# Long convolutions by quarters: fewer transform products, with sums, differences and gates on GpSimd

## The reference, cut to what matters

```
u = dwconv3(h @ w_in, conv_w, conv_b)              # 512 x 3072
v, x1, x2 = split(u)
filt = (sin-MLP(positions) @ f_w3) * decay         # forward and backward filters
k2 = concat(fwd, 0, reversed bwd); k2 /= sum(|k2|)
zc = v
for o in range(2):                                  # two orders
    y  = irfft(rfft(zc, n=1024) * rfft(k2[o]))[:512]
    zc = gates[o] * (y + skip[o] * zc)
out = zc @ w_out
```

## Time and profile before

| what | value |
|---|---|
| median of the runs shown | 2739.63 us |
| the profiled execution: its own time, its span | 2741.72 us, 2739.7 us |
| TensorE busy | 2678.6 us (98%) |
| VectorE busy | 1723.7 us (63%) |
| ScalarE busy | 1024.8 us (37%) |
| GpSimd busy | 136.6 us (5%) |

### The profile page before, as it was taken

How to read it: one execution, slowest core, us unless ns; L and a number is a source line. 1 busy time by engine, 2 the same in 40 slices (tenths; PEclk the granted TensorE clock), 3 DMA queues, 4 the chain that set the end, 5 groups by cost and what they waited for, 6 DMA issues and landing times.

```text
span 2739.7 us, 35605 instructions
## 1 busy us (share of the span) xinstructions
PE 2678.6 (98%) x14500; PEld 2158.4 (79%) x14500; DVE 1723.7 (63%) x2544; ACT 1024.8 (37%) x1488; POOL 136.6 (5%) x171
## 2 busy tenths in 40 slices
PE   8999899999998999999899999999999999999999
PEld 6777688888775688888775788888888888888888
DVE  4388677474677567574757567575664988644434
ACT  4355444232435444242427543232432223432323
POOL 0000200000033200000003200000000000000000
PEclk9999999999999999999999999999999999999999
DMA  4432144343321134343220046454231111332221
GB/s 173 118 76 66 48 134 148 128 138 96 91 89 62 51 128 149 118 150 98 89 89 1 32 135 204 150 186 137 97 121 62 32 35 46 102 114 93 92 86 53
DMA packets 247210, 275.27 MB, mean 100 GB/s; under 512 B 9287, under 2 KB 213575, under 8 KB 247048
## 3 DMA queue, kind: packets, MB, share of 16 engines
q1 hardware_dynamic: 216696, 217.67, 24.9%
q10 hardware_dynamic: 30352, 55.31, 6.3%
HBM read 265.36 MB, written 7.34 MB: 100 GB/s over the span
## 4 chain that ended last, share of the span: by engine, by line
PE 87%; DVE 8%; ACT 3%; issue 2%; DMA 0%; ACTq 0%; DVEq 0%
PE ps L571 24%; PE ps L573 23%; PE ps L572 23%; PE ps L1291 3%; PE ps L1323 2%; PE ps L1044 2%; PE ps L1061 1%; PE ps L1248 1%; DVE sb L2407 1%; DVE sb L2405 1%; PE ps L1269 1%; DVE sb L1983 1%; PE ps L1158 1%; PE ps L1078 1%; PE ps L630 1%
## 5 line engine op out<-in xcount | busy, mean ns | idle before, releaser
L571 PE MATMUL ps<-sb 128*128 128x512 f32 (+1 forms) x3332 | 1256.7, 377 | 14.3 <-ACT sb L1449 3.1
L573 PE MATMUL ps<-sb 128*128 128x512 f32 (+1 forms) x3332 | 1235.7, 371 | 0.0
L572 PE MATMUL ps<-sb 128*128 128x512 f32 (+1 forms) x3332 | 1235.4, 371 | 0.0
L571 PEld LDWEIGHTS ps<-sb 128*128 128x128 f32 x3332 | 628.0, 188 | 145.0 <-issue 27.8
L573 PEld LDWEIGHTS ps<-sb 128*128 128x128 f32 x3332 | 628.2, 189 | 108.7
L572 PEld LDWEIGHTS ps<-sb 128*128 128x128 f32 x3332 | 628.6, 189 | 104.9 <-issue 1.4
L1983 DVE TENSOR_TENSOR sb<-sb 128x2048 fp32r<-128x2048 f32 (+1 forms) x185 | 413.8, 2237 | 318.7 <-ACT sb L1409 318.7
L1409 ACT ACTIVATE sb<-sb 128x2048 fp32r<-128x2048 f32 (+1 forms) x193 | 359.7, 1864 | 269.0 <-PE ps L573 267.4
L2269 DVE SCALAR_TENSOR_TENSOR sb<-ps,sb 128x511 f32<-128x511 f32 (+1 forms) x264 | 193.6, 747 | 126.5 <-ACT sb L1664 121.3
L1664 ACT ACTIVATE sb<-ps,sb 128x512 f32<-128x512 f32 x132 | 96.1, 778 | 273.8 <-PE ps L573 268.1
L2305 DVE SCALAR_TENSOR_TENSOR sb<-sb 128x512 f32<-128x512 f32 x168 | 126.0, 750 | 12.9 <-DVE sb L2302 0.5
(11 more groups left out here) (245 smaller groups left out, 2164.5 us busy)
## 6 DMA issues: line engine op xcount, KB each, us to landing
sb<-in_ffn_w_up SPq DMA_DIRECT2D x88, 1024.0 KB, 4.9
sb<-in_ada_w ACTq DMA_DIRECT2D x192, 256.0 KB, 3.2
sb<-in_ffn_w_down SPq DMA_DIRECT2D x32, 1024.0 KB, 4.9
sb<-in_ffn_w_down SPq DMA_DIRECT2D x16, 768.0 KB, 4.5
sb<-in_hy_w_in SPq DMA_DIRECT2D x12, 1024.0 KB, 4.9
sb<-in_hgrn_w_in SPq DMA_DIRECT2D x8, 1024.0 KB, 5.9
sb<-in_hgrn_w_in SPq DMA_DIRECT2D x16, 512.0 KB, 4.5
sb<-in_dsa_w_in SPq DMA_DIRECT2D x7, 1024.0 KB, 5.1
```

The costliest lines, as they stand in the source:

```text
L571: pe.matmul(o, al, bh, start=f, stop=False, **kw)
L572: pe.matmul(o, ah, bl, start=False, stop=False, **kw)
L573: m = pe.matmul(o, ah, bh, start=False, stop=l, **kw)
```

## The change

The tokens are now kept in four quarters (tokens 0, 2, 1, 3 modulo 4), and the transforms of the even tokens are made for the first 128 frequencies alone: one bank for tokens 0 mod 4, one for tokens 2 mod 4. The sum of the two quarters serves frequency half 0, the difference half 1. Four products make the even banks, eight the odd ones, 12 in all instead of 16. The sum and the difference are made by GpSimd in SBUF, from ScalarE's copies of the two banks, and VectorE's `transform` waits for them. GpSimd also takes over the second step of `sizes` and the multiplication by the gate (for i below 7), and its program is written out as a chain in which each instruction waits for the one before. On ScalarE `skip(i)` is moved behind the copies of KK and of the tokens.

```diff
@@ PE
-                def transform(name, i, ft, srcs):
+                def transform(name, i, srcs):
+                    for t in range(2):
+                        b = transform_banks(name, i, t)[0]
+                        wait_bank(b)
+                        for sine in range(2):
+                            m = pe.matmul(ps[b][:, 256 * sine:256 * sine + 256], direct(t, sine), sdz(i, srcs[sine])[:, t, :], start=True, stop=True)
+                        m.then_inc(*mark("pe_hy", (name + "_mm", i, t, 0)))
+                        freed[b] = [(name, i, t, "even")]
+                    for ft in range(2):
+                        b = transform_banks(name, i, ft)[1]
+                        wait_bank(b)
+                        for sine in range(2):
+                            one = direct(2, 1 - sine) if ft else direct(2, sine)
+                            three = other(sine) if ft else direct(3, sine)
+                            o = ps[b][:, 256 * sine:256 * sine + 256]
+                            pe.matmul(o, one, sdz(i, srcs[sine])[:, 2, :], start=True, stop=False)
+                            m = pe.matmul(o, three, sdz(i, srcs[sine])[:, 3, :], start=False, stop=True)
+                        m.then_inc(*mark("pe_hy", (name + "_mm", i, ft, 1)))
@@ ACT
                 for i in range(8):
-                    transform("XX", i, 0)
+                    transform("XX", i)
                     if i < 7:
                         filter_sizes(i + 1)
-                    transform("XX", i, 1)
+                    if i < 7:
+                        transform("KK", i + 1)
+                        tokens(i + 1)
                     skip(i)
@@ DVE sizes
-                    dve.wait_ge(*at("sizes_0", i))
-                    dve.tensor_tensor(Y.sizes[:, 0:2], Y.sizes[:, 0:2], Y.sizes[:, 2:4], ADD).then_inc(*mark("dve_hy", ("sizes", i)))
@@ DVE transform
-                    dve.wait_ge(*at(name, i, ft, "even"))
+                    dve.wait_ge(*at("difference" if ft else "sum", name, i))
@@ DVE invert
-                        g = 8 * (o + 1) + j
-                        dve.wait_ge(*at("u", g))
-                        dve.tensor_tensor(Y.u[:, j, :], t[:, :], Y.u[:, g, :], MUL)
+                        if i == 7:
+                            ...
@@ POOL
+                def transform(name, i):
+                    e = even_parts(name, i)
+                    for t in range(2):
+                        pool.wait_ge(*at(name, i, t, "even"))
...
+                    pool.tensor_tensor(e[:, 0, :], Y.ef[0][:, :], Y.ef[1][:, :], ADD).then_inc(*mark("pool_hy", ("sum", name, i)))
+                    behind("difference", name, i)
+                    pool.tensor_tensor(e[:, 1, :], Y.ef[0][:, :], Y.ef[1][:, :], SUB).then_inc(*mark("pool_hy", ("difference", name, i)))
+                negated(0)
+                sizes(0)
+                transform("KK", 0)
+                negated(1)
                 for i in range(8):
+                    transform("XX", i)
+                    if i < 7:
+                        sizes(i + 1)
+                        transform("KK", i + 1)
+                    if i:
+                        gated(i - 1)
+                    if i + 2 < 8:
+                        negated(i + 2)
```

More of the change, by code:

```diff
@@ L147, in shape_constants @@
     c["perm"] = perm
-    order = np.concatenate([np.arange(0, L, 2), np.arange(1, L, 2)])
+    order = np.concatenate([np.arange(r, L, 4) for r in (0, 2, 1, 3)])
     tl = np.linspace(0.0, 1.0, L, dtype=f32)
@@ L509, in norm_bank, with even_parts @@
             return 2 if i else 4
+        def even_parts(name, i):
+            return Y.even[name] if name == "XX" or i else Y.even_first
         def sdz(i, w):
@@ L1286, in transform @@
                         wait_bank(b)
[L1287 to L1292, removed]
@@ L1293, in transform @@
-                        freed[b] = [(name, i, ft, "even" if half == 0 else "all")]
-                def filter_transform(i, ft):
+                        for sine in range(2):
[12 more added lines that the diff above has]
+                        m.then_inc(*mark("pe_hy", (name + "_mm", i, ft, 1)))
+                        freed[b] = [(name, i, ft, "all")]
@@ L1352, in hyena @@
                     elif c == 10:
[L1353 to L1354 removed]
+                        filter_transform(0)
                 filters(1)
@@ L1359, in hyena @@
                         pe.wait_ge(*at("z", i, half))
-                    for ft in range(2):
-                        transform("XX", i, ft, (2, 2))
+                    transform("XX", i, (2, 2))
                     if i < 7:
@@ L1864, in filter_sizes @@
                     m.then_inc(*mark("act_hy", ("abs", i)))
[L1866 to L1873, removed]
+                last_parts = [None]
+                def transform(name, i):
+                    for t in range(2):
+                        act.wait_ge(*at(name + "_mm", i, t, 0))
+                        if t == 0 and last_parts[0]:
+                            act.wait_ge(*at(*last_parts[0]))
+                        act.copy(Y.ef[t][:, :], ps[transform_banks(name, i, t)[0]][:, :]).then_inc(*mark("act_hy", (name, i, t, "even")))
+                    last_parts[0] = ("difference", name, i)
                 def tokens(i):
@@ L2792, in hyena, with behind, negated @@
                 pool.memset(Y.aT[64:128, 0:1], 0.0).then_inc(*mark("pool_hy", ("delayed",)))
[L2793 to L2795 removed]
+                last = [("delayed",)]
+                def behind(*event):
+                    pool.wait_ge(*at(*last[0]))
+                    last[0] = event
+                def negated(i):
+                    pool.wait_ge(*at("w3", i))
+                    behind("negated", i)
+                    pool.tensor_scalar(Y.w3[64:128, 256:512], Y.w3[64:128, 256:512], -1.0, None, MUL).then_inc(*mark("pool_hy", ("negated", i)))
@@ new lines, in sizes, with transform @@
+                def sizes(i):
+                    pool.wait_ge(*at("sizes_0", i))
+                    behind("sizes", i)
+                    pool.tensor_tensor(Y.sizes[:, 0:2], Y.sizes[:, 0:2], Y.sizes[:, 2:4], ADD).then_inc(*mark("pool_hy", ("sizes", i)))
+                def transform(name, i):
+                    e = even_parts(name, i)
+                    for t in range(2):
+                        pool.wait_ge(*at(name, i, t, "even"))
+                    if name == "KK" and i == 0:
+                        pool.wait_ge(*at("used", ("hy", "in", 10)))
+                    elif i == 0 or (name == "KK" and i == 1):
+                        pool.wait_ge(*at("used", ("hy", "in", 11)))
+                    else:
+                        for ft in range(2):
+                            pool.wait_ge(*at(name, i - 1, ft, "all"))
+                    behind("sum", name, i)
+                    pool.tensor_tensor(e[:, 0, :], Y.ef[0][:, :], Y.ef[1][:, :], ADD).then_inc(*mark("pool_hy", ("sum", name, i)))
+                    behind("difference", name, i)
+                    pool.tensor_tensor(e[:, 1, :], Y.ef[0][:, :], Y.ef[1][:, :], SUB).then_inc(*mark("pool_hy", ("difference", name, i)))
@@ new lines, in gated @@
+                def gated(i):
+                    o, cq = divmod(i, 4)
+                    for ct in range(2):
+                        j = 2 * cq + ct
+                        g = 8 * (o + 1) + j
+                        pool.wait_ge(*at("conv_read", i, ct))
+                        pool.wait_ge(*at("u", g))
+                        behind("uo", i, ct)
+                        pool.tensor_tensor(Y.u[:, j, :], Y.tv[ct][:, :], Y.u[:, g, :], MUL).then_inc(
+                            *mark("pool_hy", ("uo", i, ct), *([("u_out", j)] if o == 0 else [])))
```

52 lines of the change are left out of this document (31 added, 21 removed).

## The result

The changed kernel takes 2787.98 us (median of 4 runs, 2783.75 to 2791.01) against 2739.9 us: a ratio of 1.0177 (95% interval 1.0164 to 1.0189), 48 us slower. The direction was forecast (slower), but not the size: 13.8 us were forecast, to 2753.4 us, and the time lies above the range (2739 to 2773).

What follows compares the result with a forecast made beforehand. TensorE alone was taken to bound each turn. Turn starts shift -1.7 us at first, +2.7 after i = 1, then +11.7 over i = 2 to 5, -0.3 twice at the end: +13.8, 2753.4 us; range 2739 to 2773.

Steps and rivals of the forecast that it cites:

- What bounds, and what is removed: TensorE alone sets a turn, 26.18 us; 12 products instead of 16 save 1.73 us per transform call, 27.6 us without waits.
- GpSimd's price and taking turns: GpSimd's two-input instructions take 1.27 us, plus the rest of VectorE's instruction where that also needs a second SBUF input.
- The two waits: TensorE stands still 3.7 us before the column sums (sizes) and 2.6 us before the filters (sign change behind gates).
- rival 1: The clock falls in TensorE's waits, 2 us lost per fall, +14 to +26 us: 2767 to 2780 us; chance 15%.
- i = 0: First loop turn, without inversion or gates: 19.5 us as before, so no loss.
- i = 1: Second loop turn, bound by VectorE in its first part; the start of the next turn goes from -1.7 to +2.7 us.
- T: Start of a turn's XX transform on TensorE, from which the forecast counts its times.
- The tail: Turn i = 7 to the last inversion, which waits for VectorE's chain: about 19.1 us, before 19.38, a gain of 0.3.
- KK of filter 0: Transform in the projections before the loop: saves 1.7 us, so the first turn starts that much earlier.

Runs made afterwards that it cites:

- a1: Changed kernel with useless products filling TensorE's waits, 8 before the column sums and 6 before the filters' product: 2761.06 us.
- b1: Changed kernel with only the second step of the sizes back on VectorE, the sign change still behind the gates: 2769.18 us.
- a2: Changed kernel with the sign change of the filter weights ahead of KK's sum and the gates in GpSimd's order: 2757.33 us.
- c2: Changed kernel with the gates back on VectorE and nothing else: 2759.3 us.
- b2: Kernel before the change with only the second step of the sizes moved to GpSimd: 2752.8 us.
- c1: Changed kernel with half of a1's filling, 4 useless products before the column sums and 3 before the filters: 2769.78 us.
- b3: Changed kernel without the second step of the sizes, column sums behind the inversion, sign change first on GpSimd, filters' PSUM banks reordered: 2732.27 us.
- c3: The same kernel as b3, run again as the measure for c4: 2733.12 us.
- a3: Changed kernel with the sign change first on GpSimd and the second step of the sizes back on VectorE: 2740.67 us.
- c4: b3 with 12 useless products on TensorE before the last inversion: 2730.89 us.
- a4: Changed kernel with the sign change first on GpSimd and TensorE's column sums behind the inversion, sizes still on GpSimd: 2747.51 us.

## Why the prediction was wrong

- **What bounds, and what is removed:** right. A transform takes 5.18 us (2223.02 to 2228.20) and not 6.91, so 12 products save 1.73 us a call, and TensorE with its waits decided the turns.
- **GpSimd's price and taking turns:** right. 1.27 to 1.28 us for each of the 16 sums (the differences are longer where they meet VectorE's products, up to 2.13), 2.18 at the sizes where it waits for L2646 (forecast 2.34 from the request to the end), 0.69 us for VectorE's PSUM-reading L2611 beside the gates.
- **The two waits:** right in place, cause and size: 3.40 for 3.7 us, 2.87 for 2.6. Without the falls a full turn of the changed kernel is 34.4 less 3.4 less 1.7 = 29.3 us, and 29.4 in a1; forecast 29.1. Undoing the one cause (b1) shortens just the first wait, to 1.88 us; undoing the other (a2, c2) takes away just the second.
- **The step that failed: the clock.** The sum priced the waits at their length, with TensorE at full rate behind them. I had the fall as rival 1 with 15%, at 2 us each and 14 to 26 us in all, and argued against it that 13 us of dense work stand between the waits. By my own sums it was 14.1 us from the first wait to the second, but only 8.6 (3.44 + 5.18) from the second to the next first; and in either case it does not protect: the clock falls after both waits in each turn from i = 2 to 5. The prices are 3.4 us behind the first (column sums and inversion 11.4 instead of 8.0) and 1.7 to 1.8 behind the second (5.40 us for filters of 3.60 to 3.70), so the 2 us of rival 1 were too little for the one and about right for the other. The whole is 27 us by a1 (the last inversion's fall not counted), where the falls alone were taken away, and about 1 more, which a1's idle products cost in i = 0. Even rival 1 came out 8 to 21 us short (2767 to 2780, against 2788), from this, from i = 0 and from the tail.
- **i = 0:** forecast at no loss, 23.4 us measured against 19.5. Its column sums show the wait of 3.4 us, which was forecast, and a fall behind it, which was not (the even banks of KK take 3.76 us, not 1.89). With the falls taken away it is still 22.6: 1.1 us of it are a1's idle products, and 1.7 us are KK's difference and the sign change, which I had counted at their lengths alone although without an inversion they meet VectorE's products.
- **i = 1:** 31.0 us against a forecast of 31.6, which is luck. I had its column sums wait for VectorE, 11.4 us after T; they start 8.76 after it, released by GpSimd's size step as in the other turns. The rest of the turn takes 22.3 us for 20.2, mostly by the fall. Without the falls the turn is 29.4.
- **The tail:** forecast a gain of 0.3 us, measured 22.1 against 19.4, and then 8.83 us for the last inversion. The chain of VectorE is 3 us later: GpSimd's last gates meet VectorE's low parts of the weights (4.72 us for two gates), ScalarE's skip and high parts wait for the gates, VectorE's low parts for ScalarE. I had followed that chain without the gates' waits. That the gates are the cause is shown by c2: with them on VectorE the tail is 19.45 us and the last inversion 7.14.
- **What stays open:** the sum of these (turns +45.7, last inversion +1.7, KK of filter 0 -1.7) is 45.7 of 48 us; the other two lie within the scatter of the changed kernel's runs (7 us). The start of the loop scatters as well: 2114.16 us in the trace of the changed kernel against 2119.59, and 2115.81 in b2, which saves no products. Why the clock falls after the same wait in one turn and not in another (1.7 us in c1, 1.15 in b3 and c3), and why the stretch at the lower level is 1.7 us dear in one turn and over 3 in another (a2, b1), was not tried apart.

## What to carry to other kernels

Where TensorE is the bound, price a new wait not by its length alone, but with the slow work behind it: here waits of 3.4 and 2.9 us cost 6.8 and 4.6. Before moving work to GpSimd, ask for each piece who waits for it and what stands behind it in GpSimd's queue: one 0.85 us sign change behind two gates, and one 1.3 us addition in front of the column sums, cost 47 us together (2788.0 against 2740.7 in a3). Even then, of a saving of 27.6 us in TensorE's work, no run kept more than 9 (c4). Idle products in a wait are a cheap test of how much of a loss is the clock.

## What the runs showed of the hardware

- The granted clock fell to 0.50 in otherwise dense work. Told by the slower work behind the wait, it fell behind every wait of 3.4 us (changed kernel, a2, c2), behind 2.9 us in four of five turns (changed kernel), behind 2.65 to 3.0 us in four of five (a4), behind waits of 1.7 to 1.95 us before the column sums in two to four of the five turns from 2170 us on (a3, b1, c1), behind 1.57 us before the filters in none of five (c1), behind 1.45 us in two of seven (b2), behind 1.15 us in b3 and c4 and not in c3, and behind 0.3 us in none (a1).
- Filling the waits with products whose results nobody reads kept it at 1.00 and was worth 27 us (a1).
- A GpSimd instruction that meets a VectorE instruction with two SBUF inputs makes both wait: 2.18 us for 1.27 (L2828), and 2.17 for 1.23 beside it (L2648). The Trainium skill (SBUF — State Buffer, the section Who interferes with whom) calls it a lock for the whole instruction taken by whoever issues first; L2646 began 0.16 us ahead of GpSimd's L2828 and kept its 1.22 us, so these rows agree.
